# Two of the last norm's eight chunks are scaled by GpSimd and finished by VectorE in one step

## What is computed

```python
def layer_norm(x, g, b):
    xf = x.astype(F32)
    mu = jnp.mean(xf, axis=-1, keepdims=True)
    var = jnp.mean(jnp.square(xf - mu), axis=-1, keepdims=True)
    y = (xf - mu) * lax.rsqrt(var + LN_EPS) * g.astype(F32) + b.astype(F32)
    return y.astype(x.dtype)
# in hybrid_layer
    x = layer_norm(ALPHA * x + f, p['ln2_g'], p['ln2_b'])
```

## Time and profile before

| | |
|---|---|
| median of 3 runs | 824.3 us (824.23 to 824.31) |
| profiled execution, own time | 824.56 us |
| its span, first to last instruction | 822.8 us |
| TensorE busy | 805.0 us (98%) |
| VectorE busy | 465.1 us (57%) |
| ScalarE busy | 166.1 us (20%) |
| GpSimd busy | 93.1 us (11%) |
| TensorE's granted clock, mean | 0.997 |

### The profile page before, as it was taken

One profiled execution on the slowest core, in us unless ns is written; L12 is line 12 of the kernel. 1 busy time (PEld: TensorE's weight loads), 2 busy tenths in 40 slices (PEclk: granted clock), 3 DMA queues, 4 the chain that ended last, 5 costly groups with the idle time before them and its releaser, 6 DMA issues.

```text
span 822.8 us, 11931 instructions
## 1 busy us (share of the span) xinstructions
PE 805.0 (98%) x4283; PEld 500.9 (61%) x4283; DVE 465.1 (57%) x1178; ACT 166.1 (20%) x275; POOL 93.1 (11%) x105
## 2 busy tenths in 40 slices
PE   9999999999999999999999999999999999999995
PEld 7876788888788888544545445454544445445443
DVE  6989899999741367533434334443444434334356
ACT  2210112111221005321211212121121212112126
POOL 1119700000010002100000000000000000000021
PEclk9999999999999999999999999999999999999998
DMA  9432344445489946699999999999999999999981
GB/s 333 151 128 103 122 139 149 155 154 115 142 321 417 414 182 249 219 397 416 423 423 420 423 425 424 422 427 420 425 425 423 424 426 424 420 424 419 419 351 53
DMA packets 45372, 262.15 MB, mean 319 GB/s; under 512 B 9928, under 2 KB 10696, under 8 KB 26256
## 3 DMA queue, kind: packets, MB, share of 16 engines
q1 hardware_dynamic: 40720, 252.88, 76.6%
q0 software_dynamic: 4608, 8.66, 2.8%
HBM read 267.10 MB, written 2.53 MB: 328 GB/s over the span
## 4 chain that ended last, share of the span: by engine, by line
PE 83%; DMA 9%; SPq 6%; DVE 1%; issue 1%; ACT 1%; ACTq 0%; DVEq 0%
PE banks L1263 35%; PE banks L1474 21%; PE banks L1518 10%; PE banks L1435 6%; DMA high<-w_gu 5%; SPq L464 4%; DMA ring<-w_gu 4%; PE banks L1410 3%; SPq L472 2%; PE banks L1364 1%; PE banks L1278 1%; PE banks L1495 1%; PE banks L1290 1%; PE banks L1440 1%; DMA ring<-w_front 1%
## 5 line engine op out<-in xcount | busy, mean ns | idle before, releaser
L1474 PE MATMUL banks<-high,low 128*64 128x512 f32 x848 | 230.1, 593 | 0.9 <-DMA high<-w_gu 0.9
L1263 PE MATMUL banks<-xT,ring 128*128 128x264 f32 x768 | 176.3, 389 | 0.3 <-DMA ring<-w_front 0.3
L1170 DVE TENSOR_TENSOR cgb<-cgb,banks 128x264 f32<-128x264 f32 x248 | 89.8, 423 | 132.1 <-PE banks L1435 131.9
L1263 PEld LDWEIGHTS banks<-xT,ring 128*128 128x128 f32 x768 | 144.5, 190 | 30.4 <-issue 5.5
L1474 PEld LDWEIGHTS banks<-high,low 128*64 128x64 f32 x848 | 73.6, 137 | 138.6 <-issue 135.1
L1222 DVE SCALAR_TENSOR_TENSOR y_pair<-banks,sml,y_pair 128x1024 fp32r<-128x1024 f32 x31 | 39.8, 1284 | 121.8 <-ACT y_pair L725 121.8
L1474 PE MATMUL banks<-ring,low 128*64 128x512 f32 x176 | 77.6, 593 | 3.0 <-DMA ring<-w_gu 3.0
L562 POOL DMA_INDIRECT low<-x_rows_dram,idx x32 | 31.9, 997 | 423.5 <-DVE idx L1114 403.0
L1435 PEld LDWEIGHTS banks<-sw,y_pair 128*128 128x128 f32 x496 | 63.0, 188 | 24.9 <-issue 23.5
L1518 PE MATMUL banks<-high,mu 128*64 128x512 f32 x336 | 77.0, 599 | 0.7 <-ACT mu L705 0.7
L1435 PE MATMUL banks<-sw,y_pair 128*128 128x264 f32 x496 | 71.1, 293 | 0.0
(11 more groups left out here) (300 smaller groups left out, 859.9 us busy)
## 6 DMA issues: line engine op xcount, KB each, us to landing
high<-w_gu SPq DMA_DIRECT2D x35, 2048.0 KB, 24.0
high<-w_dn SPq DMA_DIRECT2D x40, 1024.0 KB, 21.9
ring<-w_front SPq DMA_DIRECT2D x78, 512.0 KB, 3.2
high<-w_gu SPq DMA_DIRECT2D x34, 1024.0 KB, 11.5
ring<-w_gu SPq DMA_DIRECT2D x7, 2048.0 KB, 28.8
us<-w_dn SPq DMA_DIRECT2D x11, 1024.0 KB, 21.8
ring<-w_gu SPq DMA_DIRECT2D x8, 1024.0 KB, 12.0
bgb<-w_dn SPq DMA_DIRECT2D x6, 1024.0 KB, 21.4
```

The costliest lines, as they stand in the source:

```text
L1170: dve.tensor_tensor(acc[:, n], acc[:, n], psum[:, bank, 0:T], ALU.add).then_inc(added, 1)
L1263: ins = pe.matmul(psum[:, 6 + n % 2, 0:T], ring[:, n % RING, k], rhs[:, k], start=(k == 0), stop=(k == KC - 1))
L1474: ins = pe.matmul(psum[SL * j:SL * j + SL, GU_BANK, :], xg[:, k, SL * j:SL * j + SL], gu[slots[j]][:, k], start=(k == 0), stop=(k == KC - 1))
```

## The change

The tail's eight scalings are divided. VectorE increments a new semaphore `last_deviation` as soon as the deviation is there, and scales chunks 0 to 5 as before. GpSimd waits for that semaphore, and multiplies chunks 7 and 6, in this order, by the deviation only. After its six, VectorE waits for each of these two products (`y_divided`), and applies weight and bias to it in one operation with one tensor input and two per-partition scalars (`y_finished`). ScalarE adds the bias to chunks 0 to 5 only. SyncE's fourth store waits for the two `y_finished` instead of for eight `y_ready`; the other three wait as before.

```diff
+        POOL_SCALED = (7, 6)
+        y_divided = sem("y_divided")
+        last_deviation = sem("last_deviation")
+        y_finished = sem("y_finished")
  # SyncE
                 for h in range(KC // 2):
-                    sp.wait_ge(y_ready, 2 * h + 2)
+                    if 2 * h in POOL_SCALED:
+                        sp.wait_ge(y_finished, len(POOL_SCALED))
+                    else:
+                        sp.wait_ge(y_ready, 2 * h + 2)
                     sp.dma_start(o_y[:, 2 * h:2 * h + 2], x1[:, 2 * h:2 * h + 2]).then_inc(stored, 16)
  # GpSimd, at its end
+                pool.wait_ge(last_deviation, 1)
+                for n in POOL_SCALED:
+                    pool.tensor_tensor(x1[:, n], acc[:, n], mu[:, 0], ALU.mult).then_inc(y_divided, 1)
  # ScalarE
                 squares(1, acc)
-                for n in range(KC):
+                for n in range(KC - len(POOL_SCALED)):
                     act.wait_ge(y_scaled, n + 1)
                     act.activation(x1[:, n], x1[:, n], ACT.Identity, bias=vec[:, V_LN + 3 * KC + n:V_LN + 3 * KC + n + 1]).then_inc(y_ready, 1)
  # VectorE
                 deviation(1)
-                for n in range(KC):
+                dve.sem_inc(last_deviation, 1)
+                for n in range(KC - len(POOL_SCALED)):
                     dve.scalar_tensor_tensor(x1[:, n], acc[:, n], vec[:, V_LN + 2 * KC + n:V_LN + 2 * KC + n + 1], mu[:, 0], ALU.mult, ALU.mult).then_inc(y_scaled, 1)
+                for i, n in enumerate(POOL_SCALED):
+                    dve.wait_ge(y_divided, i + 1)
+                    dve.tensor_scalar(x1[:, n], x1[:, n], vec[:, V_LN + 2 * KC + n:V_LN + 2 * KC + n + 1], vec[:, V_LN + 3 * KC + n:V_LN + 3 * KC + n + 1], ALU.mult, ALU.add).then_inc(y_finished, 1)
```

## The result

The changed kernel takes 825.32 us (median of 22 runs), the kernel before 824.20 in as many: +1.12 us, a ratio of 1.0013 with a 95% interval of 1.0007 to 1.0019. That is slower, clear of the noise by the interval, and within the 0.2% that I had called "same". Forecast were 825.1 and a range of 823.9 to 825.8.

What follows compares the result with a forecast made beforehand. The end was taken as bound by VectorE's scaling rate and then the last store's landing. Increment 0.08, interference 0.98 and store 0.40 behind the third gave +0.65, queueing +0.15: +0.80, 825.1 us by the median, range 823.9 to 825.8.

Steps and rivals of the forecast that it cites:

- The increment: VectorE's semaphore increment between deviation and first scaling: delays all that follows by 0.08 us, bounds 0.02 and 0.13.
- The interference: VectorE's two-SBUF-input scalings beside GpSimd's reading products: 0.98 us lost, 1.46 at most; likeliest case, chance 0.66.
- The row at 19.3: Earlier trace, GpSimd negating a table for 3.55 us: one VectorE product lost 0.71, a fifth; applied to the pair, 0.3.
- The finishing operations: VectorE's two last weight-and-bias operations: 0.35 each, 0.27 apart, up to 0.15 more each; end 820.49, off the path.
- The stores' issues: SyncE at the end: third store at 820.55, fourth 0.40 behind (0.36 to 0.46) at 820.95, +0.65 against before.
- The queueing: Fourth store waiting in the DMA engines behind the third store's bytes: +0.15 us, within 0 to 0.3.
- 87% busy: DMA engines from 818.6 to 821.8: stores need at least 2.8 of 3.2 us, so at most 0.4 can be won.
- A: Rival, scalings beside products: no or small interference, fourth store 0.33 earlier, 824.0 to 824.3, say 824.1; chance 0.21.
- B: Rival: GpSimd held off until the sixth scaling ends, store at 820.80, +0.5, 824.8 us; chance 0.06.
- C: Rival: GpSimd's multiplication dearer than its addition, 1.09 us per product, 826.2 to 826.5, slower by over 0.2%; chance 0.04.
- GpSimd's drain: GpSimd's end-of-block drain, 2.7 us past its last operation: through by 821.5, hidden, 0.9 before the last store lands.
- D: Rival: the rest of the kernel changes through other placing of instructions or transfers, either sign; chance 0.03.

Runs made afterwards that it cites:

- e1: Kernel before plus only the semaphore increment ahead of the eight scalings; span ends 7.04 us after the third deviation step starts, before 6.91.
- e2: Changed kernel, deviation written a second time to PSUM by VectorE and read there by its six scalings; span ends at +7.44 us, changed kernel +7.95.
- e3: Changed kernel with GpSimd's two products replaced by fills that write SBUF and read nothing; span ends at +6.98 us, changed +7.95, before +6.91.
- e11: Changed kernel with GpSimd copying chunks 7 and 6 onto themselves instead of multiplying; span ends at +7.26 us, changed kernel +7.95.
- e4: Changed kernel with only chunk 7 on GpSimd, seven scalings and biases on VectorE and ScalarE; span ends at +7.46 us, changed kernel +7.95.
- e6: Changed kernel with the third store cut to 8 columns of its two chunks; span ends at +7.83 us, changed kernel +7.95.
- e12: Changed kernel with GpSimd's products started only after VectorE's second scaling; span ends at +7.91 us, changed kernel +7.95.
- e5: Changed kernel with GpSimd's products held until all six scalings are done; span ends at +7.75 us, changed kernel +7.95.
- e9: Arithmetic of e7 with four two-chunk stores, three by SyncE, chunks 4-5 by ScalarE; 824.42 us against 824.38 before, ratio 0.9999.
- e7: Changed kernel, ScalarE copying deviation to PSUM for scalings 2-5, GpSimd after first scaling, no separate increment, eight one-chunk stores; 824.59 us, ratio to before 1.0003.
- e8: Kernel before with eight stores of one chunk each, nothing else; 824.70 us against 824.41 before, ratio 1.0004.

## Why the prediction was right, step by step

**The increment.** Taken at 0.08 (0.02 to 0.13), it is 0.13 (e1), the upper bound. The row after the scans had said 0.15 from end to start against 0.02 without an increment, and I had no reason to go below it.

**The interference, the term that decided.** Taken at 0.98, it is (0.997 - 0.484) + (0.969 - 0.484) = 1.00. The kind was right, shown by e2 (one input moved to PSUM: nothing) and e3 (GpSimd writes only: nothing). The size came out of a share that is not as general as I used it. Two thirds of GpSimd's time held for the products (0.51 of 0.74) but e11 gives 0.16 of 0.40 for a copy, two fifths. It was a hit on the nearest row, with luck. I had said the loss falls in the first three or four scalings; it is in the first two, one per product. So the first store already bears all of it.

What carries over better than a share is who started first. The instructions of the changed kernel one by one (timeline):

```profile
816.88 0.74 POOL L604 TENSOR_TENSOR cgb<-cgb,mu 128x264 f32<-128x264 f32 x1 [3.56 <-DVEq L1255]
816.91 1.00 DVE L1257 SCALAR_TENSOR_TENSOR cgb<-cgb,vec,mu 128x264 f32<-128x264 f32 x1 [0.17 <-DVE mu L1047]
...
817.58 0.93 POOL L604 TENSOR_TENSOR cgb<-cgb,mu 128x264 f32<-128x264 f32 x1
...
817.83 0.97 DVE L1257 SCALAR_TENSOR_TENSOR cgb<-cgb,vec,mu 128x264 f32<-128x264 f32 x1
```

An instruction that starts while one of the other engine runs is the one that gets longer. Take from its end the length that it has alone (0.484 for a scaling, 0.74 for a product, 0.40 for a copy), and there is the moment from which it goes at full speed. For a scaling this is 0.19 to 0.20 us before the end of GpSimd's instruction, in all nine slowed scalings of the changed kernel, e4, e6, e11 and e12, for products and copies alike. For a GpSimd instruction it is 0.14 before the end of the scaling, in all eight cases. So they take turns, and the loss is what is left of the other's instruction, less a fixed piece. For a copy of 0.40 the fixed piece counts for more, which gives two fifths instead of two thirds. By the same reckoning the piece is 0.13 in the earlier trace rows, where the VectorE operations have 32 columns, and 0.25 for the finishing operation of e5. What sets it is open. The row at 19.3 does not follow: the product there was held for 0.71 and ended 0.66 before GpSimd's 3.55 did.

The rule of the Trainium skill ("SBUF — State Buffer", section "Who interferes with whom") that I set against the rows agrees with the traces in which pairs meet: two SBUF inputs against a reading GpSimd do (1.00 us), one input in SBUF and one in PSUM (e2) and a GpSimd that only writes (e3) don't. Taken literally it has the loser blocked for the other's whole instruction, and that gave 1.46; measured is 1.00, mainly because each of the two waits ends 0.19 us before the end of the instruction waited for.

**The finishing operations.** Priced at 0.35 each and 0.27 apart, they are 0.406 and 0.33 apart, within the bound of 0.15 more. They end at +4.77, while the last store is issued at +5.06. They are off the path, as said.

**The stores' issues.** Third store: expected 1.06 later than before, measured 4.69 - 3.57 = 1.12. Fourth: 0.375 behind it where I took 0.40; +0.68 in all, expected +0.65.

**The queueing, the term that was mis-sized.** Taken at 0.15 within 0 to 0.3, it is 2.42 - 2.06 = 0.36, beyond its bound. By e6, 0.24 of it is the bytes ahead, which the bound had room for, and 0.12 is the longer issue of a store right behind another (0.456 instead of 0.332), which the sum didn't have at all. With it the tail is 7.95 - 6.91 = 1.04 longer, where the sum had 0.80; the missing 0.24 is nearly all this. The reason is the reading of the earlier trace rows: "87% busy" I took as 13% to be won. It is not. From first packet to last the stores take 3.27 us before, and 3.14 in the changed kernel and in e3: 0.13 was to be won, not 0.4. In stretches of 3.2 us the three move 333, 334 and 338 GB/s, though the issues are spread over 2.4 us before and 2.0 in the other two. A pair needs 0.75 to 0.8 us, and the stores of before, 0.81 apart, already came at about that pace. With pairs bunched at the end, the span ended 3.25 to 3.28 after the third store's issue in the changed kernel, e2, e3, e4, e11 and e12, and 3.42 in e9, where the fourth was issued only 0.08 behind it; before, with the fourth 0.81 behind, it ended 3.34 after. That the third store rather than the first counts was tested by e12.

**The rivals.** A was priced at 824.1, a gain of 0.2. Its price was wrong: e3 is that case, its fourth store goes out 0.31 earlier, nearly as said, and its tail is 0.07 longer than before, because the landing takes 0.38 more. B (GpSimd held off until the last scaling) didn't occur, but e5 builds it: priced at +0.5, measured 7.75 - 6.91 = +0.84; the difference is made of small steps, nearly all of it of three: 0.05 more for the increment, 0.14 from the last scaling's end to GpSimd's start, which I had at nothing, and 0.48 instead of 0.35 from the last product's end to that of the last finishing operation. The slowing of the first finishing operation (0.41), which I had not thought of, is nearly hidden: the second had to wait for GpSimd's second product until +4.70 anyway, and started at +4.77. C falls with the product's 0.74. GpSimd's drain was hidden, as said: the store lands later. D, another placing of the rest, has nothing for it: the tail alone accounts for 1.04 of the 1.12.

The median moved by 1.12, the tail of the profiled executions by 1.04. The remaining 0.08 is well inside the spread of the runs (824.77 to 826.03).

## What to carry to other kernels

Before work is moved from VectorE to GpSimd, look at both instructions' operands: with two SBUF inputs on VectorE and reads on GpSimd, here two products cost VectorE 1.00 us where the two operations taken off it were worth 0.81, and two new ones came in their place. Starting GpSimd later doesn't help by itself: in e12 the scaling under way kept its length, and the next two lost 0.98. A PSUM copy of the shared operand removed that loss entirely (e2), but cost VectorE 0.48 us itself; ScalarE made it in e7 without delaying the scalings. At the end of a kernel, ask first what the last two stores need to move: while that is the bound, a last store issued 0.73 us earlier ended the kernel no earlier (e9), and only a delay of the stores ahead of it shows.

## What was not expected of the hardware

- A VectorE operation with one tensor input and two per-partition scalars is slowed beside a GpSimd product as well: 0.816 instead of 0.405 us (e5).
- SyncE's issue of a store of one or two whole chunks takes 0.33 to 0.35 us when it has been idle and 0.40 to 0.50 when it follows another at once; the last six of eight were 0.49 apart (e8), and that made small stores dearer than large ones.
- The waiting goes both ways, by turns: a GpSimd product that starts during a scaling takes 0.93 instead of 0.74 us (the changed kernel, e7), and the wait of either engine ends a fixed piece before the other's instruction does, 0.19 to 0.20 or 0.14 us.
- GpSimd's drain at the end of the block ends 2.71 us after its last instruction in all fourteen profiles, whether that was an add, a fill, a copy or a product.
